# A ring of ten weight units, skipped padding rows and an accumulating scatter in the expert stage of a decoder step

## The reference

```python
def hier_moe(x, p):                                   # x: 520 rows of 1024
    p1 = softmax(x @ w_router1 + b_router1)           # 4 groups, the best one is taken
    l2 = (x @ w_router2 + b_router2)[group]           # 8 experts in it, the best two are taken
    top_w = softmax(top_2(l2)) * top1_p
    for each of 32 experts:
        h = silu(x @ w_gate[e]) * (x @ w_up[e]) * combine[:, e]     # 1024 -> 512
        y = y + h @ w_down[e]                                       # 512 -> 1024
y = h + hier_moe(rmsnorm(h, g_ffn))
```

## Time and profile before

| | |
|---|---|
| three runs | 1293.37, 1296.27, 1298.17 us |
| median | 1296.27 us |
| span of the profiled execution | 1288.5 us (its own time is not listed apart; the runs lie 4.9 to 9.7 us above the span) |
| PE busy | 1060.3 us, 82% |
| DVE busy | 458.5 us, 36% |
| ACT busy | 175.3 us, 14% |
| POOL busy | 71.2 us, 6% |
| moved | 294.33 MB, mean 228 GB/s |

### The profile page before, as it was taken

One profiled execution on the slowest core, in us unless ns is written; L12 is line 12 of the kernel. 1 busy time (PEld: TensorE's weight loads), 2 busy tenths in 40 slices (PEclk: granted clock), 3 DMA queues, 4 the chain that ended last, 5 costly groups with the idle time before them and its releaser, 6 DMA issues. The chain is left out here.

```text
span 1288.5 us, 16001 instructions
## 1 busy us (share of the span) xinstructions
PE 1060.3 (82%) x6275; PEld 694.2 (54%) x6275; DVE 458.5 (36%) x950; ACT 175.3 (14%) x415; POOL 71.2 (6%) x104
## 2 busy tenths in 40 slices
PE   5899979999996899988996498788887788877880
PEld 2455657777784677776455354444444444444440
DVE  3233313422424678653434322222222222222223
ACT  1021211111100344330001000000000000000000
POOL 0000030100100000000000100000000000000003
PEclk9999889999976799686996698999999999999995
DMA  9970083553100600004115279999999999999995
GB/s 396 266 231 25 13 199 99 154 141 98 50 1 2 253 1 1 1 1 196 69 63 231 81 284 401 403 400 408 409 404 407 405 407 410 406 413 415 407 382 207
DMA packets 58438, 294.33 MB, mean 228 GB/s; under 512 B 6992, under 2 KB 23183, under 8 KB 40783
## 3 DMA queue, kind: packets, MB, share of 16 engines
q1 hardware_dynamic: 35191, 255.76, 51.8%
q0 software_dynamic: 5280, 21.15, 5.2%
q10 hardware_dynamic: 17920, 16.78, 4.2%
HBM read 272.55 MB, written 25.42 MB: 231 GB/s over the span
## 5 line engine op out<-in xcount | busy, mean ns | idle before, releaser
L1751 PE MATMUL ps<-w_b,xTe 128*64 128x256 f32 x1024 | 132.0, 416 | 37.8 <-DMA w_b<-in_w_up 34.1
L1751 PE MATMUL ps<-w_a,xTe 128*64 128x256 f32 x1024 | 123.2, 397 | 27.0 <-DMA w_a<-in_w_up 24.9
L1813 DVE COPY xTe<-ps 128x512 f32<-128x512 f32 x32 | 22.1, 692 | 345.9 <-PE ps L1741 345.9
L829 PE MATMUL ps<-XT,w_a 128*128 128x126 f32 (+1 forms) x576 | 132.9, 409 | 5.7 <-DVE ht L564 5.7
L829 PEld LDWEIGHTS ps<-XT,w_a 128*128 128x128 f32 x576 | 120.4, 227 | 15.4 <-issue 6.3
L1751 PEld LDWEIGHTS ps<-w_b,xTe 128*64 128x64 f32 x1024 | 81.4, 150 | 83.9 <-DMA w_b<-in_w_up 40.9
L1751 PEld LDWEIGHTS ps<-w_a,xTe 128*64 128x64 f32 x1024 | 74.3, 142 | 71.3 <-DMA w_a<-in_w_up 30.8
L430 PE MATMUL ps<-w_b,xT 128*128 128x454 f32 (+1 forms) x240 | 81.1, 549 | 0.7 <-ACT z L402 0.7
L1856 ACT ACTIVATE gc<-gc 128x256 f32<-128x256 f32 x32 | 13.3, 416 | 450.2 <-DVE gc L1819 450.2
L1726 POOL DMA_INDIRECT xg<-hn_dram,table x32 | 28.8, 899 | 592.6 <-PE ps L1741 453.9
L1378 PE MATMUL ps<-w_b,mT 128*128 128x512 f32 x128 | 58.1, 614 | 1.9 <-ACT mT L1446 1.3
(11 more groups left out here) (362 smaller groups left out, 1308.5 us busy)
## 6 DMA issues: line engine op xcount, KB each, us to landing
w_a<-in_w_gate SPq DMA_DIRECT2D x16, 2048.0 KB, 17.2
w_a<-in_w_up SPq DMA_DIRECT2D x16, 2048.0 KB, 23.3
w_a<-in_w_down SPq DMA_DIRECT2D x16, 2048.0 KB, 12.5
w_b<-in_w_gate SPq DMA_DIRECT2D x16, 2048.0 KB, 16.6
w_b<-in_w_up SPq DMA_DIRECT2D x16, 2048.0 KB, 22.4
w_b<-in_w_down SPq DMA_DIRECT2D x16, 2048.0 KB, 13.2
w_a<-in_cache_kv SPq DMA_DIRECT2D x64, 256.0 KB, 5.1
ys_dram<-yb ACTq DMA_DIRECT2D x64, 128.0 KB, 7.8
```

The lines of the kernel that those rows point to most:

```text
L829: ins = nc.tensor.matmul(hidv[:, 2 * q:2 * q + 2, 0:n], w1[:, q, l, :], XT[:, q, :, l:l + 8 * (n - 1) + 1:8], start=(l == 0), stop=(l == 15))
L1751: ins = nc.tensor.matmul(ps[h * CAP:h * CAP + CAP, bank, 0:FH], xT[:, slot, k, :], w[slot][:, k, h * FH:h * FH + FH], start=(k == 0), stop ...
L1813: nc.vector.tensor_copy(xT[:, slot, :, :].rearrange("p k s -> p (k s)"), ps[:, 4, 0:KD * CAP]).then_inc(xT_ready, 1)
```

## The change

- **Ring.** The weights are cut into 96 units (gate, up, down of each expert). Ten places hold them: three in `w_a`, three in `w_b`, two in the memory of `z`, two new ones (`more`). Unit u goes to place u mod 10 when PE has done the product that used unit u-10. For `z` to be free in `mix`, POOL first copies its `u` columns to `zu`.
- **Two transfers each.** A unit comes in two transfers of 1 MiB with a semaphore each, and PE waits for the first half, multiplies, and waits for the second.
- **Start.** `mix` loads units 0, 1, 2, 6, 7 at its start, 3 and 4 at its last tile, 5 at its end. Units 8 and 9 are issued as soon as `experts` starts. The first two gathers move into `mix`.
- **Padding.** Unused slots hold a number beyond the last token, and the transfers leave such rows out (slot 0 of each tile always holds some token, with weight 0 if unused). PE, DVE and ACT still compute all 64 slots.
- **Scatter.** `mix` stores `h` straight to the output `y`. PE's table product also gives the weight of each slot (`slot_w`), ACT multiplies by it in its copy, and POOL adds the result rows to `y` with an accumulating indirect transfer, the next one only when the one before has landed, since a token's two experts may follow each other. `ys_dram`, its zeros, `h_dram`, `combine` and the separate `overflow` stage go.
- **No loops.** The 32 experts are written out on all engines.

The core of the difference (array views and the overflow part, which does not run here, are cut):

```diff
+UNIT = KD * FF
+RING = 10
@@ project, POOL and SP
-            nc.gpsimd.memset(blank[:, :], 0.0).then_inc(blank_ready, 1)
-            pool.dma_start(self.ys_dram[NEXP * CAP:, :]..., blank[:, :]...).then_inc(self.blanked, 16)
-            sp.wait_ge(self.blanked, 16)
@@ mix, SP
-            self.load_gate_up(sp, 0, 0, (wg, wu))
-            self.load_down(sp, 0, 0, wd)
+            for u in range(3):
+                self.load_unit(sp, u)
+            sp.wait_ge(u_kept, 2)
+            for u in range(6, 8):
+                self.load_unit(sp, u)
...
-                sp.dma_start(self.h_dram[t * P:t * P + r, :], h[0:r, t % 2, :]).then_inc(stored[t % 2], 16)
+                sp.dma_start(O["y"][t * P:t * P + r, :], h[0:r, t % 2, :]).then_inc(stored[t % 2], 16)
@@ mix, POOL
+            nc.gpsimd.tensor_copy(zu[:, 0:TILES, :], z[:, 0:TILES, U0:U0 + 256]).then_inc(u_kept, 1)
+            nc.gpsimd.tensor_copy(zu[0:NB, TILES, :], z[0:NB, TILES, U0:U0 + 256]).then_inc(u_kept, 1)
...
+            pool.wait_ge(table_ready, 1)
...
+            for n in range(2):
+                self.gather(pool, n)
@@ mix, PE
-                    ins = nc.tensor.matmul(ps[0:CAP, 0, 0:NTILE], slot_hot[0:r, n, :], tile_tok[0:r, n, :], ...)
+                    for a in range(2):
+                        ins = nc.tensor.matmul(ps[CAP * a:CAP * a + CAP, 0, 0:2 * NTILE], slot_hot[0:r, n, :], tile_hot[0:r, n, :, :]..., ...)
@@ experts, SP
+            for u in range(8, NU):
+                if u >= RING:
+                    n, m = (u - RING) // 3, (u - RING) % 3
+                    if m == 0:
+                        sp.wait_ge(gate_done, 2 * n + 2)
+                    elif m == 1:
+                        sp.wait_ge(up_done, 2 * n + 2)
+                    else:
+                        sp.wait_ge(y_in_psum, 2 * n + 2)
+                self.load_unit(sp, u)
@@ experts, POOL
             for n in range(NEXP):
-                if n >= 2:
-                    pool.wait_ge(x_turned, n - 1)
-                pool.indirect_dma_start(out=xg[:, n % 2, :], ...).then_inc(xg_in[n % 2], 16)
+                if n + 2 < NEXP:
+                    pool.wait_ge(x_turned, n + 1)
+                    self.gather(pool, n + 2)
+                pool.wait_ge(y_copied, n + 1)
+                if n >= 1:
+                    pool.wait_ge(y_out, 16 * n)
+                scatter(pool, n, n % 2, y_out)
@@ experts, PE
-                    pe.wait_ge(sem[slot], half * 16)
                     for k in range(KD):
+                        if k % 4 == 0:
+                            arrived(3 * n + m, k // 4)
```

More of the change, by code:

```diff
@@ L1676, in load_down @@
-    def load_down(self, sp, n, slot, w):
-        src = self.ins["w_down"].rearrange("(e h p j) d -> e p h j d", h=2, p=P, j=KF // 2)
-        sp.dma_start(w, src[bass.ds(n, 1), :, :, :, :].rearrange("e p h j d -> (e p) h j d")).then_inc(self.weights_in[2][slot], 16)
+            row = junk[:, 0:NTILE]
+            dve.wait_ge(mixed_ready, NT)
+            ch.then(nc.vector.tensor_scalar(row, ps[:, 0, 0:NTILE], float(FAR), self.c(C_LAST, 1), ALU.add, ALU.min))
+            nc.vector.tensor_copy(self.table[:, :], row[0:CAP, :]).then_inc(table_ready, 1)
@@ L1690, in experts @@
         FH = FF // 2
-        wg, wu, wd = zip(self.expert_slot(self.w_a), self.expert_slot(self.w_b))
-        xg = self.sb("xg", [CAP, 2, D], stack=st)
+        more = self.sb("more", [P, RING - 8, UNIT], stack=st)
+        self.units += [more[:, j, :] for j in range(RING - 8)]
         xT = self.sb("xTe", [P, 2, KD, CAP], stack=st)
-        gc = self.sb("gc", [2 * CAP, 2, FF // 2], stack=st)
-        hh = self.sb("hh", [2 * CAP, 2, FF // 2], stack=st)
+        gc = self.sb("gc", [2 * CAP, 2, FH], stack=st)
@@ L1705, in experts, with needed, scatter @@
+        def needed(eng):
+            return eng.If(eng.value_load(self.n_over[0:1, 0:1], min_val=0, max_val=NOVER) > 0)
+        def scatter(pool, n, slot, sem):
+            pool.indirect_dma_start(out=rows, out_offset=bass.IndirectOffsetOnAxis(ap=self.halves[:, n:n + 1].bitcast(U32), axis=0),
+                                    in_=yb[:, slot, :], in_offset=None, bounds_check=2 * NTOK - 1, oob_is_err=False,
+                                    compute_op=ALU.add).then_inc(sem, 16)
         block = st.enter_context(nc.Block("experts"))
@@ L1794, in _ @@
-            n, half = NEXP - 2, NEXP // 2
-            gate_up(n, 0, half)
-            turn_x(n + 1, 1, half)
-            down(n - 1, 1, half - 1)
-            turn_h(n, 0)
-            gate_up(n + 1, 1, half)
-            down(n, 0, half)
-            turn_h(n + 1, 1)
-            down(n + 1, 1, half)
+                turn(5, hh[:, n % 2, :], KF // 2).then_inc(h_turned, 1)
+            turn_x(0)
+            for n in range(NEXP):
+                gate_up(n)
+                if n + 1 < NEXP:
+                    turn_x(n + 1)
+                if n >= 1:
+                    down(n - 1)
+                turn_h(n)
@@ L1995, in _ @@
+                if n >= 2:
+                    act.wait_ge(y_out, 16 * (n - 1))
+                nc.scalar.activation(yb[:, n % 2, :], ps[0:2 * CAP, 6 + n % 2, :], ACT.Copy, scale=self.slot_w[:, n:n + 1]).then_inc(y_copied, 1)
+            exp(0)
+            for n in range(1, NEXP):
+                exp(n)
+                take_y(n - 1)
+            take_y(NEXP - 1)
             with needed(act):
+                act.wait_ge(y_out, 16 * NEXP)
                 with act.Fori(0, NOVER) as j:
-                    act.wait_ge(gc_ready, j + 1)
```

475 lines of the change are left out of this document (185 added, 290 removed).

## The result

The changed kernel takes 1385.12 us (median of 4 runs, 1378.91 to 1390.13) where the kernel before takes 1297.22 on the same chip: a ratio of 1.0661, 95% interval 1.0603 to 1.0719. It is 6.6% slower; 1244 was forecast, and the range ended at 1288. The profiled run took 1378.91 us, its span is 1377.1. Ratios are to the kernel before on the same chip, whose medians lie from 1292.5 to 1304.2 us over the experiments. One of its executions, at 2369.41 us beside gather first, is a slow one and not counted.

What follows compares the result with a forecast made beforehand. The weight stream was taken as the bound, 16.72 us per expert. Start +3.3, units already there -22.3, 28 x 0.32 = -9.0 and the end -24.6 gave 1244 us, range 1224 to 1288.

Steps and rivals of the forecast that it cites:

- rival 1: POOL issues scatter n before gather n+3, closing a loop through the down product that sets the pace; chance 0.09.
- 7.4 + L: One round of POOL's loop: 7.4 us of copy, wake, scatter issue, wake, turn and down, plus the landing.
- L: Landing time of the gathered rows in POOL's loop: 6.5 to 7.7 us expected, loss from 9.7.
- The rule of packet by packet: DMA engines go round their queues packet by packet, which would put the gather's landing below 8.8 us.
- Bytes per expert: Weights, gather and scatter of one expert in the stream: 6.69 MB, 16.4 us, from 16.07 to 17.05.
- D: Time from the end of the first down product to the end of the last: forecast at 467.7 us.
- Rival 2: Accumulate or small packets cost engine time: 14 to 18 us more, 1258 to 1262 us; chance 0.12.
- Two units already there: Weights of expert 2 in at the first down's end: 12 units landed, 84 left for 88, -22.3 us.
- The start: Everything up to the end of the first down product: +3.3 us, from 756.0 to 759.3.
- The end: Behind the last down product at 1227.0: copy, wake, last scatter, branch and closing, 9 us, to 1236.0.
- (3): Waits for weight halves lower PE's clock, so PE bounds at 17.3 us per expert, 1312 us; chance 0.03.
- (4): Instructions written out for all experts instead of looped cost 1 to 2 us, inside the range.

Runs made afterwards that it cites:

- gather first: Changed kernel with POOL issuing the gather of expert n+3 ahead of the scatter of expert n: 1260.55 us, ratio 0.9708.
- the filler kernels: Changed kernel plus 40 or 20 unread PE products per expert before the wait for gathered rows: 1456.88 us with 40, 1338.31 us with 20.

## Why the prediction was wrong

The failed step is in rival 1, and it is a size: the round 7.4 + L of POOL's loop. With "I expect 6.5 to 7.7" for L it came to at most 15.1 us, below the stream's 16.4, and rival 1 got a chance of 0.09. Once around was named in full and in the right order; the mechanism is the one that the runs show. Measured, the round takes 20.3: L came out at 10.1, and the terms outside L at 3.4 more than 7.4, most of it the down product behind PE's own wait.

The formula's point of loss, L = 9.7, was too low as well: it has 42 us for the last three experts, and they took 29.4 (the scatters of expert 28 and 31 start at 1336.6 and 1366.0), since the very last down product follows the one before it in 4.7 us. With 29.4 there, L = 10.1, the 7.4 as it stood and the measured start and end, the sum is 762.7 + 28 x 17.5 + 29.4 + 12.7 + 1.8 = 1297, the time of the kernel before. The mis-sized L alone takes the forecast from 1244 to no change; what the round takes beyond 17.5 makes the 82 us from there to the 1379 of the profiled run.

- **How L was put together.** "3.7 unloaded, and of the 5.1 us that the load adds now half, plus up to 1.4 for the scatter." Half for half the rows: all 64 rows land in 10.8, so the rows give 0.7. Weights in halves do help, 12.2 to 10.1. The scatter beside it was to cost 1.4 at most; its adding alone costs 2.2. Beside that, a plain scatter with half the rows and smaller weight rows leaves 7.9, where these two alone should have made 8.8 into 8.8 - 0.7 - 2.1 = 6.0. That the rest, 1.9 us, is a second small transfer in the same queue is argued, not shown.
- **The rule of packet by packet.** By the Trainium skill, page "DMA: Bandwidth & Descriptors", section "Queues, rings and completion order", an engine goes round its queues, and I took it to mean an L below 8.8. The kernel with one transfer per unit agrees in sign (longer neighbour rows, landing 12.2 for 10.1), but the rule gives no size; 8.8 was not beaten until the adding was gone (7.9).
- **The rest of the round.** Copy 0.65 was 0.69 and the turn 1.38 was 1.42. The wake, 0.27, was 0.82. The scatter's issue, 1.25 from 128-row gathers, was 1.85 to the next instruction. From the gather's start to PE's turn it was 9.69. Down, 3.65, was 5.73, and 5.81 to ACT's start, since PE's wait lowers the granted clock; the filler kernels show it. Together, for 7.4 + L: 0.04 + 0.55 + 0.60 + 0.04 + 2.16 = 3.4 us more outside L, so that even with the L of 10.1 the formula gives 17.5 where the round takes 20.3 (20.4 in the mean). I had treated the clock as a rival of its own instead of a result of this one.
- **Bytes per expert.** D was forecast at 467.7 with 9 us in it for the adding, so 458.5 without. Measured, it is 478.7 with gather first and 464.2 with a plain scatter as well: the adding was 5.3 too low, and another 5.7 are there without it. The two kernels that reorder the refills take 5.9 off D together, so most of the 5.7 is likely the hole that SP's order leaves; that is argued. In the full stretch the pace was right: 6.557 MB at the 400 GB/s of gather first are 16.4 us, and at the 408 of the plain scatter 16.07.
- **Rival 2.** Its 1258 to 1262 us meets the 1260.55 of the kernel without the loop by luck. It put 14 to 18 us into the experts, where D has 11.0; the profiled run is 1244 + 8.6 (first down product at 767.9, for what lies ahead of `mix` above all) + 11.0 + 3.6 (end) - 6.0 = 1261.2, and took 1261.0. Its small packets cost nothing: 408 GB/s as in the earlier trace rows.
- **Two units already there, 12 in at the first down product.** By the ring of eight two of them are worth 8.9 us of D. What I missed is SP's order: 12 blocks 13 and 14, and "SP issues three units at every end of a down product, so the queue stays full" holds only behind the first few experts.
- **The start.** 759.3 was 762.7; by the way from the start of `mix`, 180.4 for 175.2 before, the change added 5.2 us where I had 3.3. POOL's copies keep PE's first product 1.5 us behind the start of the stage (583.80 for 582.28), as the 1.6 allowed; the product itself takes 1.94 for 1.06. The table product took 3.66 for 2.53, +1.1 where I took 2.3. The barrier behind the two gathers keeps PE until 730.23, 6.8 us behind the table product (5.8 before), and the 1.5 us that the gathers in `mix` were to save are not seen.
- **The end.** Nine us behind the last down product were 12.7: ACT's copy, 0.78 to POOL's start, 1.55 of issue, then 9.6 from there to the end. The 31.7 us of the earlier trace rows became 12.7 all the same, the gain that `combine` was to give.
- **From span to median.** I added 7.8 us, from other runs' medians; each run here lies 1.8 above its own span. By parts for the profiled run: 1244 + 3.4 (start) + 134.0 (D) + 3.7 (end) - 6.0 = 1379.1, and it took 1378.9.
- **Rivals.** PE as the bound through its waits for halves (3) did not come: with gather first the granted clock is 1.00 and 0.94, and the stream sets the pace at a share of 1.02. Single waits for halves were longer than the 0.8 us that I had, up to 2.7. Code written out (4): 0.2% of the engines' time as before.

## What to carry to other kernels

Where an engine issues in order, write out every ring that its waits close, instruction by instruction, and put into it the landing time under load with its worst row, not one scaled by bytes: a small transfer behind a full stream takes what its neighbours make it take, here 7.9 to 12.9 us. Then ask what a wait in that ring does to the clock of the engine that waits. Issue first what waits for the earlier event: gathers ahead of the scatter, refills in the order in which their places come free.

## What the runs showed of the hardware

- The landing of a small gather beside the weight stream: 10.8 us with 64 rows of 4 KB, 10.1 with 32; 12.2 with gate and up in rows of 16 KB and one transfer per unit, 10.1 with rows of 8 KB and two; 7.9 when the scatters in the same queue overwrite instead of add. Halving the bytes is the weakest of the three.
- An accumulating indirect transfer of about 65 half rows of 2 KB costs POOL 1.55 us to issue where a plain one costs 1.01, lands in a median of 9.8 us beside the stream where the plain one takes 7.1, and its adding takes 0.4 to 0.5 us of all engines' time.
- 28 waits of 6 us, one every 20 us, put the granted clock at 0.84 (0.50 for 6.5 us around the down product of the round shown) and made the down product take 5.0 to 5.9 us instead of 3.65. With 4.5 us of each wait filled by products that nobody reads the clock was 1.00 up to 1190 us and the kernel 3.4% faster; behind waits of 1.5 to 2.4 us after that it was 0.92 and the product 5.1 to 5.4.
